# Attention scores of two heads in one group of 64-row matmuls, narrower scores on the diagonal, and two merge units moved into attention

## The reference

```python
h = rms_norm(x, norm_mix)
q, k, v, u, g_a, g_p = split(h @ w_in)
q, k = rope(rms_norm(q)), rope(rms_norm(k))            # per head
gate = q . mean(k over each block of 256)              # only blocks fully past
sel  = the 3 blocks with the largest gate              # per token and head
p    = softmax over [own block, causal] + [selected blocks], scores * 64**-0.5
o_attn = p @ v
o_pool = multiscale_pool(u)
merged = sigmoid(g_a) * (o_attn @ w_up_attn) + sigmoid(g_p) * (o_pool @ w_up_pool)
x = x + merged @ w_out
x = x + relu(rms_norm(x) @ w_ff1)**2 @ w_ff2
```

## Time and profile before

| what | value |
|---|---|
| median of 3 runs | 955.9 us (954.8 to 956.35) |
| the profiled execution: its time | 953.49 us |
| its span, on the slowest core (core 7) | 952.4 us |
| spans of the 8 cores | 947.3 to 952.4 us |
| PE busy | 913.4 us, 96% of the span |
| PEld busy | 469.2 us, 49% |
| DVE busy | 461.5 us, 48% |
| ACT busy | 381.0 us, 40% |
| POOL busy | 75.3 us, 8% |

### The profile page before, as it was taken

One profiled execution on the slowest core, in us unless ns is written; L12 is line 12 of the kernel. 1 busy time (PEld: TensorE's weight loads), 2 busy tenths in 40 slices (PEclk: granted clock), 3 DMA queues, 4 the chain that ended last, 5 costly groups with the idle time before them and its releaser, 6 DMA issues.

```text
span 952.4 us, 17253 instructions; the slowest of 8 cores (947.3 to 952.4 us)
## 1 busy us (share of the span) xinstructions
PE 913.4 (96%) x5772; PEld 469.2 (49%) x5772; DVE 461.5 (48%) x876; ACT 381.0 (40%) x738; POOL 75.3 (8%) x133
## 2 busy tenths in 40 slices
PE   3798999899999999999999999999999999999997
PEld 1344555667767764444444444444444444444443
DVE  2578877555532333434775444434444444444443
ACT  2566666798899982222004344031111221111120
POOL 4212110321000000100001000000000000000000
PEclk9899999999999999999999999999999999999999
DMA  8942023523433337793989904250064100001113
GB/s 196 212 121 68 2 73 89 85 44 76 65 65 63 68 59 130 155 216 79 194 131 154 140 1 57 36 86 1 1 89 59 31 1 1 1 0 77 60 64 155
DMA packets 57895, 76.31 MB, mean 80 GB/s; under 512 B 27792, under 2 KB 46224, under 8 KB 57552
## 3 DMA queue, kind: packets, MB, share of 16 engines
q0 software_dynamic: 24288, 40.28, 27.5%
q1 hardware_dynamic: 33520, 34.92, 13.5%
HBM read 98.41 MB, written 8.39 MB: 112 GB/s over the span
## 4 chain that ended last, share of the span: by engine, by line
PE 87%; DMA 6%; DVE 3%; issue 2%; ACT 1%; SPq 0%; POOL 0%; DVEq 0%; ACTq 0%; POOLq 0%
PE bank L1339 23%; PE bank L1313 23%; PE bank L986 10%; PE bank L429 8%; PE bank L880 6%; PE bank L1223 6%; PE bank L918 3%; PE bank L1000 3%; PE bank L1005 3%; DMA raw<-w_qkvu 3%; DMA raw<-x 2%; DMA raw<-w_slice 1%; PE bank L483 1%; DVE raw L399 0%; DVE raw L457 0%
## 5 line engine op out<-in xcount | busy, mean ns | idle before, releaser
L1320 ACT ACTIVATE raw<-bank 128x512 f32<-128x512 f32 x128 | 76.4, 597 | 375.8 <-PE bank L1313 317.2
L1313 PE MATMUL bank<-raw 128*128 128x512 bf16 x1024 | 223.1, 379 | 0.0
L1339 PE MATMUL bank<-raw 128*128 128x512 bf16 x1024 | 223.1, 379 | 0.0
L887 ACT ACTIVATE raw<-bank 128x512 bf16<-128x512 f32 x288 | 152.6, 613 | 19.3 <-PE bank L918 17.6
L1313 PEld LDWEIGHTS bank<-raw 128*128 128x128 bf16 x1024 | 100.4, 98 | 120.7
L1339 PEld LDWEIGHTS bank<-raw 128*128 128x128 bf16 x1024 | 100.0, 98 | 121.0
L1322 DVE SCALAR_TENSOR_TENSOR raw<-bank,raw 128x512 bf16<-128x512 f32 x128 | 88.5, 692 | 140.8 <-ACT raw L1320 140.7
L1345 DVE SCALAR_TENSOR_TENSOR raw<-bank,raw 128x512 f32<-128x512 f32 x128 | 96.1, 751 | 112.7 <-PE bank L1339 112.4
L429 PE MATMUL bank<-raw 128*128 128x512 bf16 x512 | 125.9, 395 | 13.5 <-DMA raw<-w_qkvu 7.6
L986 PE MATMUL bank<-raw 128*128 128x512 bf16 x512 | 122.5, 379 | 0.4 <-DMA raw<-w_slice 0.3
L880 PE MATMUL bank<-raw 128*128 128x256 bf16 x576 | 101.7, 272 | 1.8 <-ACT raw L887 1.2
(11 more groups left out here) (91 smaller groups left out, 604.1 us busy)
## 6 DMA issues: line engine op xcount, KB each, us to landing
raw<-x SPq DMA_DIRECT2D x32, 512.0 KB, 6.3
raw<-w_ff POOLq DMA_DIRECT2D x16, 1024.0 KB, 12.4
raw<-w_slice POOLq DMA_DIRECT2D x22, 640.0 KB, 8.0
out<-raw SPq DMA_DIRECT2D x16, 512.0 KB, 2.6
raw<-w_qkvu POOLq DMA_DIRECT2D x8, 512.0 KB, 12.9
raw<-raw SPq DMA_DIRECT2D x2, 1024.0 KB, 7.5
raw<-w_out POOLq DMA_DIRECT2D x4, 512.0 KB, 13.6
raw<-c_ind POOLq DMA_DIRECT2D x4, 256.0 KB, 6.2
```

Source lines behind the costliest of these rows:

```text
L887: t.op("act", lambda e: e.activation(out=pt, in_=bank_f(sb_), func=AF.Exp, scale=0.125), reads=hb[sb_], writes=[b_PT[si % NPT]])
L1313: t.group("pe", [lambda e, c=c, j=j, bk=bk: e.matmul(bank_f(bk), lhsT=ffw1[s][:, c, j * 128:(j + 1) * 128], rhs=hT[:, c, tg * 512:(tg + 1) ...
L1320: t.op("act", lambda e, bk=bk, si_=si_: e.activation(out=sqz[si_], in_=bank_f(bk), func=AF.Square), reads=hb[bk], writes=[b_sqz[si_]])
L1339: t.group("pe", [lambda e, j=j, bk=bk, hf=hf, i=i: e.matmul(bank_f(bk), lhsT=a1T[ab][:, j, i * 128:(i + 1) * 128], rhs=ffw2[s][:, j, hf * ...
```

## The change

Four things change.

1. **Order of the steps.** For each query block the steps now run over pairs of heads, and in a pair over the blocks of keys, even head first, then odd. `start` of the accumulation is set by the first head of a bank alone, as two heads of a bank now alternate.
2. **Narrower diagonal.** In a diagonal step the second 128 keys see only the second 128 queries: the second matmul has 128 columns in place of 256, the exponential 384 in place of 512, and the columns of `PT` move up accordingly. The triangle still covers 256 columns.
3. **Scores in head pairs.** Steps without a block bias (`qk_open`: `qb < 4`, or the diagonal) contract over 64 rows alone, rows 0 to 63 for the even head and 64 to 127 for the odd one. Both heads' scores are emitted at the even step as one group of four matmuls, alternating between the two banks and the two halves of the rows; then both exponentials. The odd step emits none. 112 steps are of this kind: 80 in the first four query blocks, 32 on the diagonals of the others. The group writes two banks, so it waits for the exponentials of steps `si - 3` and `si - 2`. The other 176 steps keep their 128 rows and single groups.
4. `NPT` is 6, and `N_ATT` is 16: 104 chunks, 277.5 / 104 = 2.67 steps apart, and 16 units after attention. The weight slices `w_slice` are loaded 24 times in place of 22.

```diff
--- before.py
+++ after.py
@@ -251,8 +251,8 @@
         pooledT = view(D0, [128, 4, S], BF16)
         NXS = 4
         xslot = [view(D0 + 16 * KB + i * 4 * KB, [128, D], F32) for i in range(NXS)]
-        NPT = 5
-        PT = [view(D0 + 16 * KB + i * KB, [128, 512], BF16) for i in range(NPT)]
+        NPT = 6
+        PT = [view(D0 + (16 + i if i < 5 else 29) * KB, [128, 512], BF16) for i in range(NPT)]
         o_tok = view(D0 + 21 * KB, [128, 2, 512], BF16)
         bias8 = [view(D0 + 28 * KB + i * 256, [128, 128], BF16) for i in range(2)]
         wout = view(D0 + 16 * KB, [128, 8, D], BF16)
@@ -552,7 +552,7 @@
 
 
         b_wsl = [Buf("wsl%d" % s) for s in range(3)]
-        N_ATT = 14
+        N_ATT = 16
         units = [(fc, 0) for fc in range(8)] + [(fc, 1) for fc in range(N_ATT - 8)]
         uses = [u_[0] for u_ in units]
         post_units = []
@@ -858,9 +858,10 @@
 
         steps = []
         for qb in range(NB):
-            for h in range(H):
+            for pr in range(H // 2):
                 for kp in range(qb + 1):
-                    steps.append((qb, h, kp))
+                    steps.append((qb, 2 * pr, kp))
+                    steps.append((qb, 2 * pr + 1, kp))
         NS = len(steps)
         LOOK = 4
         first_of = {}
@@ -868,26 +869,54 @@
             first_of.setdefault(qb_, i_)
         first_of[NB] = NS
 
-        def emit_qk(si):
+        def qk_open(si):
+            qb, h, kp = steps[si]
+            return qb < 4 or kp == qb
+
+        def qk_fns(si, half):
             qb, h, kp = steps[si]
             pr = h // 2
             sb_ = st_banks[si % 3]
             q0 = qb * 256
             ksel = kT if h % 2 == 0 else kT2
+            r0, r1 = ((0, 64) if h % 2 == 0 else (64, 128)) if half else (0, 128)
             fns = []
             for j in range(2):
                 kt = 2 * kp + j
-                fns.append(lambda e, kt=kt, j=j: e.matmul(
-                    bank_f(sb_)[:, j * 256:(j + 1) * 256], lhsT=ksel[:, pr, kt * 128:(kt + 1) * 128],
-                    rhs=qTz[:, h, q0:q0 + 256], start=True, stop=True))
-            rd = [b_kT[2 * kp], b_kT[2 * kp + 1], b_qT[2 * qb], b_qT[2 * qb + 1]] 
-            rd += [b_ind[pr // 2][h % 2]] + ([b_kT2h[pr // 2]] if h % 2 else [])
-            t.group("pe", fns, reads=rd, writes=hb[sb_])
+                qa = 128 if kp == qb and j == 1 else 0
+                fns.append(lambda e, kt=kt, j=j, qa=qa: e.matmul(
+                    bank_f(sb_)[:, j * 256:j * 256 + 256 - qa], lhsT=ksel[r0:r1, pr, kt * 128:(kt + 1) * 128],
+                    rhs=qTz[r0:r1, h, q0 + qa:q0 + 256], start=True, stop=True))
+            rd = [b_kT[2 * kp], b_kT[2 * kp + 1], b_qT[2 * qb], b_qT[2 * qb + 1]]
+            if not half:
+                rd.append(b_ind[pr // 2][h % 2])
+            if h % 2:
+                rd.append(b_kT2h[pr // 2])
+            return fns, rd
+
+        def emit_qk(si):
+            qb, h, kp = steps[si]
+            if not qk_open(si):
+                fns, rd = qk_fns(si, False)
+                t.group("pe", fns, reads=rd, writes=hb[st_banks[si % 3]])
+                emit_exp(si)
+            elif h % 2 == 0:
+                fa, ra = qk_fns(si, True)
+                fb, rb = qk_fns(si + 1, True)
+                t.group("pe", [fa[0], fb[0], fa[1], fb[1]], reads=ra + rb,
+                        writes=hb[st_banks[si % 3]] + hb[st_banks[(si + 1) % 3]])
+                emit_exp(si)
+                emit_exp(si + 1)
+
+        def emit_exp(si):
+            qb, h, kp = steps[si]
+            sb_ = st_banks[si % 3]
+            nc_ = 384 if kp == qb else 512
             pt = PT[si % NPT]
-            t.op("act", lambda e: e.activation(out=pt, in_=bank_f(sb_), func=AF.Exp, scale=0.125),
+            t.op("act", lambda e: e.activation(out=pt[:, 0:nc_], in_=bank_f(sb_)[:, 0:nc_], func=AF.Exp, scale=0.125),
                  reads=hb[sb_], writes=[b_PT[si % NPT]])
             if kp == qb:
-                dg = pt.rearrange("p (a c) -> p a c", c=128)[:, 0:4:3, :]
+                dg = pt.rearrange("p (a c) -> p a c", c=128)[:, 0:3:2, :]
                 if si < 80 or si in gate_busy:
                     t.op("pool", lambda e: e.affine_select(
                         out=dg, in_=dg, pattern=[[0, 2], [1, 128]],
@@ -914,10 +943,10 @@
                     last = (2 * qb) if ql == 0 else (2 * qb + 1)
                     o_ = (ql * 3 + hh) * 65
                     dst = bank_f(bk)[:, o_:o_ + 65]
-                    c0_ = j * 256 + ql * 128
+                    c0_ = j * 256 + (0 if kt == 2 * qb + 1 else ql * 128)
                     fns.append(lambda e, dst=dst, c0_=c0_, kt=kt, ql=ql, last=last: e.matmul(
                         dst, lhsT=pt[:, c0_:c0_ + 128], rhs=v_aug[:, kt, h, :],
-                        start=(kt == 0 and ql == 0), stop=(kt == last), skip_group_check=True))
+                        start=(kt == 0 and ql == 0 and hh == 0), stop=(kt == last), skip_group_check=True))
             t.group("pe", fns, reads=rds, writes=hb[bk])
             if kp == qb and (hh == 2 or h == H - 1):
                 n = hh + 1
```

## The result

The changed kernel takes 1.0124 times as long as the one before, 95% interval [1.009, 1.0157]. Its runs are 965.61, 968.79 and 969.54 us, those of before lie between 954.05 and 956.35. The forecast was 953.9 us, with a range of 947 to 962. The profiled execution took 965.61 us, 12.1 more than that of before.

A forecast was written before the change was run, and what follows sets the result against it. ScalarE was taken to bound early attention and TensorE the rest from step 46. Attention ending 8.3 us later and 10.3 us less after it gave -2.0: 951.5 us profiled, plus 2.4 for the median, 953.9 us; range 947 to 962.

The forecast's parts named there:

- What switching the array costs: TensorE changing between 128-row and 64-row matmuls: taken as 0 us a switch, though no row shows it.
- the near end: The value 0 for a switch, from a transpose between scores and a chunk; a full emptying would be 0.164 us.
- a sign of its being wrong: In the profile after, a hole of over 60 ns at the starts of the pairs would refute the prediction.
- the first rival: Each switch empties the array: 64 switches at 0.08 us, +5.1 us, 959.0 us; at 0.164, 964.4; chance 0.27.
- After attention ... at worst 1 or 2 us: Stage after attention: two units fewer, 10.3 us less; nothing added for later loads, at worst 1 or 2 us.
- the other sign named: The stage after attention falling short of its 10.3 us saving by over 2 us (loads) would refute the prediction.
- The new wait: Attention from step 46: pairs wait for a nearer exponential, 4.7 us at eight pairs, 3.2 at four, 8.4 in all.
- the 0.5 for a `tanh`: Waits of pairs in attention: a `tanh` standing between exponentials adds about 0.5 us in all.
- The TensorE sum: Attention from the first big chunk, bound by TensorE: instruction prices total 151.9 us, 3.2 more; with waits the stage lasts 163.0.
- the second rival: The halves of a pair run one after the other: +4.8 us, 960.7 us; chance 0.10.
- Ahead of step 46: Early attention, bound by ScalarE from step 28: step 46's chunk at 201.2 us, 3.3 before the old step 50.
- The narrowing: Diagonal steps: 128 fewer columns, a diagonal pair 0.16 us on TensorE, each diagonal exponential 0.106 us shorter.

The follow-up runs named there:

- units-at-14 run: The changed kernel with 14 units in attention and 18 after it, all else as changed; 963.5 us profiled, 1.0060 times the kernel before.
- the narrowing alone: The kernel before with only the narrower diagonal (128-column second score matmul, 384-column exponential); 952.8 us profiled, 0.9975 times the kernel before.

## Why the prediction was wrong

The forecast was a gain of 2.0 us against the profiled execution. By its own steps:

1. **"What switching the array costs", taken as 0: this step failed.** Its ends were 0 and 0.164 us, and the near end was chosen because a transpose between other matmuls showed no hole. That row changes the kind of matmul and keeps its 128 rows; it says nothing of a change of rows. Measured: 0.10 in and 0.11 out, above the middle of the ends, and over the 60 ns that the prediction named as a sign of its being wrong. With the tally of the first rival (64 switches, the 12 entries behind waits free, so 20 entries and 32 exits) this is 20 x 0.10 + 32 x 0.11 = 5.5 us. That rival had the mechanism and, at 0.08, 959.0 us.
2. **"After attention ... at worst 1 or 2 us": this step failed too.** It looked at the weight slices alone. The chunks that were moved away had been the cover for another load, the transposes of `o_tok` into the merge's input. Price on core 7: 3.53 us of lateness and 5.14 - 3.45 = 1.69 of low clock, 5.2 together; over the cores the stage is 4.25 longer than forecast, which was the other sign named (over 2 us). The units-at-14 run takes the whole wait away.
3. **The new wait: right.** Eight and four places were named, and eight and four it was. From the starts, the eight cost 5.3 us (0.60 to 0.69 each; forecast 0.59, together 4.7) and the four 2.9 (forecast 3.2): 8.2 for 8.4. That the sum is so close is in part luck: the eight cost 0.6 more and the four 0.3 less than forecast, and the 0.5 for a `tanh` shows nowhere by itself.
4. **The TensorE sum: right but for the switches.** The pairs ran side by side, so the second rival falls. 163.0 - 0.2 + 5.5 + 1.4 (low clock) = 169.7; core 7 took 169.8.
5. **Ahead of step 46: too good by 2.05** (39.05 for the 40.3 - 3.3 = 37.0 forecast). Pairs were credited with 1.0 here and charged 0.3; the units-at-14 run against the narrowing alone shows them, with their order, costing 2.6. The 64 rows with their switches are not the reason: the same pairs with 128 rows, which switch nothing, take 1.05 us longer in this stage (40.1 for 39.05). So the cost lies in the grouping, the order or the sixth tile; which of them was not tried. ScalarE, which was to set the pace without a gap, is busy 9.60 of 10 us at 190 to 200.
6. **The narrowing: right.** 2.05 and 0.8 us alone, where the same prices (0.05 a diagonal step, 0.106 an exponential) gave 2.1 and 0.8.

The first two steps alone carry the time over the top of the range: 953.9 + 5.5 + 4.25 = 963.7. With the low clock and the early stage, 1.4 and 2.05, it is 967.1, among the runs of 965.61 to 969.54.

## What to carry to other kernels

Price a mode by its borders: two heads in 64 rows beside each other save 0.22 us and lose 0.20 to the two switches, and with 128 columns in the second matmul (0.37 against 0.33 for the pair of 128 rows) they lose. Behind a wait the way in is free, and there such a pair gained 0.06 us. By these prices such groups pay when several stand behind each other; no run here has that. Before work is moved away from behind a stage's end, list every transfer that this work covered, and the time from its issue to its landing, not only the loads that the work itself needs. And the end taken for an unknown cost needs a row that changes the same thing; where no row does, a value between the ends is the better forecast.

## What the runs showed of the hardware

- A change from 128-row to 64-row matmuls and back costs TensorE about 0.10 us each way at 2.4 GHz, in the pairs and in single groups alike. It shows as no idle time in the rows of the matmuls. It shows in the starts, and in weight loads that begin with their matmul instead of ahead of it (263.04 and 263.31 against 262.72 for 262.82).
- A wait of 3.37 us was followed by a mean clock of 0.66 over 5 us, and 16 matmuls took 5.14 us in place of 3.45: another 1.69 us, half as much as the wait again. After waits of 2.7 and 2.8 us on three other cores the clock stayed full.
- Two transposing DMAs issued one behind the other took 7.8 (before) and 8.0 us (after) to land, while the medians of all 32 are 6.0 and 4.7. Weight slices and a load of 512 KB were in flight with them; which of these delays them was not tried.
